# Project a layer's first five units from tiles without their 1/rms factor and scale the results; let two buffer pairs change roles

## What is computed

```python
for l in range(DEPTH):
    u = rmsnorm(h, norm_g[l])                       # h * rsqrt(mean(h*h) + eps) * g
    p = u @ w_in[l]                                 # 1024 x 9216
    hq, hf_f, hf_b, hi, hgt, aq, ak, av, agt = split(p)
    o_h = hgrn2_mixer(hq, hf_f, hf_b, hi, hgt, lbs[l], hg_norm_g[l])
    o_a = diff_attention_mixer(aq, ak, av, agt, ...)
    h = h + concatenate([o_h, o_a]) @ w_out[l]      # 2048 x 1024
out = rmsnorm(h, final_norm_g)
```

## Time and profile before

| | |
|---|---|
| median of 3 runs | 1586.7 us (1586.59 to 1586.84) |
| the profiled execution, its own time | 1587.1 us |
| its span, first to last instruction | 1585.3 us |
| PE busy | 1496.3 us (94%) |
| DVE busy | 986.5 us (62%) |
| ACT busy | 772.8 us (49%) |
| POOL busy | 533.2 us (34%) |
| mean granted TensorE clock | 0.988 of full |

### The profile page before, as it was taken

How to read it: one execution, slowest core, us unless ns; L and a number is a source line. 1 busy time by engine, 2 the same in 40 slices (tenths; PEclk the granted TensorE clock), 3 DMA queues, 4 the chain that set the end, 5 groups by cost and what they waited for, 6 DMA issues and landing times.

```text
span 1585.3 us, 27727 instructions
## 1 busy us (share of the span) xinstructions
PE 1496.3 (94%) x11148; PEld 1412.5 (89%) x11148; DVE 986.5 (62%) x1542; ACT 772.8 (49%) x1689; POOL 533.2 (34%) x287
## 2 busy tenths in 40 slices
PE   5999999999999999999979999999999999999986
PEld 4999999999999999998879999999998898888874
DVE  6666677676734666666465666676676356665655
ACT  5445444554434555555434544445444345565542
POOL 2323322333333333333333333333333343333331
PEclk8999999999999999999989999999999999999999
DMA  4221111211223222222122121221212232222221
GB/s 155 81 67 55 54 58 63 68 55 54 68 68 94 68 68 68 67 65 66 59 67 75 60 67 54 67 63 58 68 54 67 67 96 79 67 71 78 74 62 66
DMA packets 34480, 109.39 MB, mean 69 GB/s; under 512 B 4912, under 2 KB 5040, under 8 KB 34352
## 3 DMA queue, kind: packets, MB, share of 16 engines
q1 hardware_dynamic: 34352, 107.61, 21.9%
HBM read 96.84 MB, written 2.10 MB: 62 GB/s over the span
## 4 chain that ended last, share of the span: by engine, by line
PE 76%; DVE 13%; issue 6%; ACT 2%; DMA 1%; POOL 1%; SPq 1%; DVEq 0%; ACTq 0%; POOLq 0%
PE proj L1247 51%; PE pair L1316 7%; PE meta L1426 3%; PE pair L1411 2%; PE pair L1413 2%; PE main L1440 2%; DVE stage L969 1%; PE main L1381 1%; DVE totals L1030 1%; PE main L1382 1%; DMA q_stack<-gate_f 1%; PE pair L1362 1%; DVE neg_max L1160 1%; DVE o_rows L1104 1%; PE main L1323 1%
## 5 line engine op out<-in xcount | busy, mean ns | idle before, releaser
L509 POOL TENSOR_TENSOR w_lo<-w_raw,w_hi 128x1024 fp32r<-128x1024 f32 x178 | 441.9, 2484 | 753.9 <-ACT w_hi L568 752.1
L1247 PE MATMUL proj<-u_hi,w_hi 128*128 128x264 f32 (+1 forms) x2048 | 497.0, 314 | 15.2 <-DVE u_lo L923 15.2
L1247 PE MATMUL proj<-u_hi,w_lo 128*128 128x264 f32 (+1 forms) x2048 | 466.8, 300 | 0.0
L1247 PE MATMUL proj<-u_lo,w_hi 128*128 128x264 f32 (+1 forms) x2048 | 466.8, 299 | 0.0
L1247 PEld LDWEIGHTS proj<-u_hi,w_hi 128*128 128x128 f32 x2048 | 329.4, 191 | 27.9 <-issue 16.3
L1247 PEld LDWEIGHTS proj<-u_hi,w_lo 128*128 128x128 f32 x2048 | 327.3, 189 | 11.1
L1247 PEld LDWEIGHTS proj<-u_lo,w_hi 128*128 128x128 f32 x2048 | 327.9, 190 | 7.6
L1160 DVE TENSOR_REDUCE neg_max<-pair 128x1 f32<-128x528 f32 (+1 forms) x144 | 101.3, 704 | 226.7 <-PE pair L1413 226.6
L743 ACT ACTIVATE decay<-pair,neg_max 128x528 f32<-128x528 f32 (+1 forms) x144 | 100.7, 699 | 253.9 <-DVE neg_max L1160 253.9
L568 ACT ACTIVATE w_hi<-w_raw 128x1024 fp32r<-128x1024 f32 x178 | 186.6, 1049 | 22.2 <-DMA w_raw<-w_units 11.9
L689 ACT ACTIVATE qk_dec<-ops 128x528 f32<-128x528 f32 (+1 forms) x112 | 75.8, 677 | 126.1 <-DVE ops L1057 126.1
(11 more groups left out here) (182 smaller groups left out, 2253.4 us busy)
## 6 DMA issues: line engine op xcount, KB each, us to landing
w_raw<-w_units SPq DMA_DIRECT2D x178, 512.0 KB, 3.5
k_stack<-k_stack SPq DMA_DIRECT2D x32, 132.0 KB, 2.3
q_stack<-gate_f SPq DMA_DIRECT2D x32, 132.0 KB, 2.4
h<-x_t SPq DMA_DIRECT2D x8, 264.0 KB, 4.7
out_t<-decay SPq DMA_DIRECT2D x4, 256.0 KB, 2.1
out_t<-ops SPq DMA_DIRECT2D x4, 256.0 KB, 2.1
cos_sin<-rope SPq DMA_DIRECT2D x1, 528.0 KB, 5.5
masks<-level_masks SPq DMA_DIRECT2D x1, 448.0 KB, 5.3
```

Source lines behind the costliest of these rows:

```text
L509: pool.tensor_tensor(w_lo[:, u % N_CUT, :, :], w_raw[:, u % N_RAW, :, :], w_hi[:, u % N_CUT, :, :].bitcast(f32), ALU.subtract)\
L1247: ins = pe.matmul(out, w, x[:, k, cols_n], start=(k == 0 and p == 0), stop=(k == last_k and p == 2))
```

## The change

The first five units of a layer take h * g, without 1/rms, as their operand. Its high and low parts are cut on ACT (`cut_raw_high`) and DVE (`cut_raw_low`) and lie in the buffers that hold the mixed heads of that layer later; the two pairs of buffers (u and mixed) change roles from layer to layer. In layer 1 the raw tiles are cut in the tail of layer 0. DVE multiplies each of the five results by 1/rms as it takes it from PSUM (`scale_first`), and ACT's sigmoids then read the staged tile (`gate_first`). The tiles of u, which units 5 and later need, are made between these steps as `FIRST_CUTS` says: two, three and three tiles behind the scaling of zb, q and v. The sum of squares moves behind piece 7 of unit 0 (layer 0) or piece 4 of unit 0 (layer 1). In layer 0 the transfers change order: gain, tile 0, weights 0, tile 1, weights 1, the other tiles, small constants; the masks and the rotary tables follow behind weights 2, under a semaphore of their own.

```diff
+FIRST_CUTS = ((), (0, 1), (2, 3, 4), (5, 6, 7), ())
+RAW_AFTER = {OUT_C: range(EARLY_TILES + 2), OUT_C + 1: (EARLY_TILES + 2,), OUT_C + 2: (EARLY_TILES + 3,)}
...
+        u_of = ((even_hi, even_lo), (odd_hi, odd_lo))
+        mix_of = ((odd_hi, odd_lo), (even_hi, even_lo))
...
+            def cut_raw_high(l, k):
...
+                wait_tile(act, l, k)
+                act.activation(mix_of[l][0][:, tile, :], h[:, tile, :], ACT.Copy, scale=g_in[:, l, tile:tile + 1])\
+                    .then_inc(raw_hi_ready, 1)
...
+            def gate_first(l, i):
...
+                if what in ("zf", "zb", "g"):
+                    use = l * HEADS * 3 + STAGE_USE[what]
+                    act.wait_ge(evacuated[t % 2], evac_count(t))
+                    a, b = (stage[:, use % 2, x, tokens(l, what)] for x in range(2))
+                    if what == "g":
+                        act.activation(a, b, ACT.Sigmoid).then_inc(first_gated, 1)
+                    else:
...
+                        w = step(act.activation(b, a, ACT.Sigmoid, scale=-1.0))
+                        act.activation(a, a, ACT.Sigmoid).then_inc(first_gated, 1)
...
+                        act.activation(ops[:, c % 2, (KF, KB)[d], :], b, ACT.Copy,
+                                       scale=one_minus_lb[:, l, row:row + 1]).then_inc(k_scaled, 1)
+                act.wait_ge(unit_done, t + 1)
+                cut_high(t + N_CUT)
...
             for k in range(KT):
+                cut_raw_high(0, k)
+                if k < 2:
+                    cut_high(k)
                 square_h(0, k)
-            cut_high(0)
+            cut_high(2)
             root(0)
...
                 for i in range(len(HG_TILES)):
-                    evacuate(l, i)
+                    gate_first(l, i)
+                    for k in FIRST_CUTS[i]:
+                        cut_u(l, k)
...
+            def cut_raw_low(l, k):
...
+                dve.scalar_tensor_tensor(raw_lo[:, tile, :], h[:, tile, :], g_in[:, l, tile:tile + 1],
+                                         raw_hi[:, tile, :].bitcast(f32), ALU.mult, ALU.subtract)\
+                    .then_inc(raw_lo_ready, 1)
...
+            def scale_first(l, i):
...
+                dve.wait_ge(unit_done, t + 1)
...
+                dve.tensor_tensor(rows_of(l, what, dst), grown(l, what, proj[t % 2]), rows_of(l, what, sq),
+                                  ALU.mult).then_inc(evacuated[t % 2], 1)
...
             for k in range(KT):
+                cut_raw_low(0, k)
+                if 1 <= k < KT - 1:
+                    add_squares(0, k)
+            prepare_exponents()
             for l in range(DEPTH):
-                norm_u(l)
...
+                invert_roots(l)
+                for i in range(len(HG_TILES)):
+                    scale_first(l, i)
+                    if l == i == 0:
+                        prepare_lower_bounds()
+                    if i == 2:
+                        follow(l, 0)
+                        follow(l, 1)
+                        start_operands(l, 0)
+                    for k in FIRST_CUTS[i]:
+                        norm_u(l, k)
+                        if k > 0:
+                            cut_u_low(l, k - 1)
+                    if i == len(HG_TILES) - 2:
+                        cut_u_low(l, KT - 1)
...
-                for k in range(KT + 1):
-                    if k < KT:
+                if l == 0:
+                    for k in range(KT):
                         piece(l, 0, k)
-                    if k > 0:
-                        piece(l, 1, k - 1)
+                        if k == KT - 1:
+                            sum_squares(l)
+                        piece(l, 1, k)
+                else:
+                    for k in range(KT):
+                        piece(l, 0, k)
+                        if k == KT // 2:
+                            sum_squares(l)
+                    for k in range(KT):
+                        piece(l, 1, k)
```

More of the change, by code:

```diff
@@ L368, in encoder_trunk, with tile_order, wait_tile @@
         dve_step = sem("dve_step")
+        def tile_order(l):
+            return TILE_ORDER if l > 0 else tuple(range(KT))
+        def wait_tile(eng, n, k):
+            tile = tile_order(n)[k]
+            if n == 0:
+                eng.wait_ge(x_in[tile], 16)
+            elif tile < EARLY_TILES - 1:
+                eng.wait_ge(last_added, (n - 1) * (EARLY_TILES - 1) + tile + 1)
+            else:
+                t = (n - 1) * LAYER_UNITS + (OUT_C if tile == EARLY_TILES - 1 else unit_of(tile))
+                eng.wait_ge(evacuated[t % 2], evac_count(t))
         halves = (slice(0, HALF), slice(HALF, T))
@@ L614, in evacuate @@
                     use = (l * HEADS + c) * 3 + STAGE_USE.get(what, 0)
-                    if what in HG_TILES and l * HG_HEADS + c > 0:
+                    if what in HG_TILES:
                         act.wait_ge(k_scaled, 2 * (l * HG_HEADS + c))
@@ new lines, in norm_u, with cut_u_low @@
+            def norm_u(l, k):
+                if k >= 4:
+                    dve.wait_ge(u_lo_ready, l * KT + k - 4 + 1)
+                dve.scalar_tensor_tensor(decay[:, k % 4, :], h[:, k, :], g_in[:, l, k:k + 1], sq[:, :],
+                                         ALU.mult, ALU.mult).then_inc(u_ready, 1)
+            def cut_u_low(l, k):
+                dve.wait_ge(u_hi_ready, l * KT + k + 1)
+                u_hi, u_lo = u_of[l]
+                dve.tensor_tensor(u_lo[:, k, :], decay[:, k % 4, :], u_hi[:, k, :].bitcast(f32), ALU.subtract)\
+                    .then_inc(u_lo_ready, 1)
@@ L1239, in piece @@
                 last_k = (EARLY_K if OUT_B <= i < OUT_LATE else KT) - 1
-                if i == 0:
-                    pe.wait_ge(u_lo_ready, l * KT + k + 1)
-                hi, lo = (mix_hi, mix_lo) if what in ("outA", "outB") else (u_hi, u_lo)
-                wh, wl = w_hi[:, t % N_CUT, k, :], w_lo[:, t % N_CUT, k, :]
+                tile = k
+                if i < len(HG_TILES):
+                    tile = tile_order(l)[k]
+                    hi, lo = mix_of[l]
+                    pe.wait_ge(raw_lo_ready, l * KT + k + 1)
+                else:
+                    hi, lo = (mix_of if what in ("outA", "outB") else u_of)[l]
+                    if i == len(HG_TILES):
+                        pe.wait_ge(u_lo_ready, l * KT + k + 1)
+                wh, wl = w_hi[:, t % N_CUT, tile, :], w_lo[:, t % N_CUT, tile, :]
                 for w, x, p in ((wh, hi, 0), (wh, lo, 1), (wl, hi, 2)):
```

146 lines of the change are left out of this document (85 added, 61 removed).

## The result

The changed kernel takes 1589.87 us (median of 16 runs, 1588.95 to 1592.55), the kernel before 1586.9 us (16 runs, 1585.44 to 1589.04). The ratio is 1.0019 with a 95% interval of 1.0011 to 1.0027: 3 us more. The profiled execution after took 1590.38 us, its span is 1588.6 us. The forecast was 1590.0 us.

A forecast was written before the change was run, and what follows sets the result against it. TensorE bound the kernel (three quarters of the last chain); VectorE's chain, held by weight cuts, would set level 1: +3.0 (layer 0) - 3.5 (layer 1) + 2 x 2.0 (clock) = +3.5 us, so 1590.0 us, range 1578 to 1595.

The forecast's parts named there:

- The holes at the heads: Head of each layer: TensorE's waits for u's low half, 8.6 us in layer 0 and 6.6 in layer 1, go.
- The opening: Start of layer 0: squares summed at 25.0, 1/rms ready at 31.35 instead of 19.0, 12.3 us later.
- The rival of a still later opening: Layer 0: 1/rms comes at 33 to 35 and all behind it moves, 1592 to 1595 us; chance 0.23.
- VectorE's chain: From 1/rms to level 1: VectorE's serial work, lengthened by weight cuts, sets level 1; layer 0 at 63.0.
- the hold: Ahead of level 1: four GpSimd weight cuts hold VectorE 2.3 us each, 9.2 in layer 0, 8.1 in layer 1.
- The rival in which VectorE isn't held: Both layers up to level 1: TensorE stays the bound, 1574 us; chance 0.10, with 0.10 more for half the holds.
- Layer 0: Up to level 1 of layer 0: level 1 at 63.0 against 60.01, 3.0 us later (bounds 1 and 5).
- the clock: Behind level 1 in each layer: TensorE's idleness lets its clock fall, adding 2.0 us (bounds 0 and 2.6).
- Layer 1: Up to level 1 of layer 1: level 1 at 857.1 against 860.61, 3.5 us earlier (bounds 1.5 and 6).
- the idleness of VectorE: Layer 1, ahead of the scaling of unit 1: 3 us VectorE can't use, since its order is written out.
- The rival in which the clock doesn't fall: Behind level 1 in both layers: no slow stretch, +3.0 - 3.5 = -0.5, 1586 us, no change; chance 0.17.
- The end: Behind level 1 and at the kernel's end: nothing changes, 0 us.

The follow-up runs named there:

- no holds: Changed kernel with GpSimd's low cuts of weight units 3 to 6 of each layer on one of eight tiles: 1577.16 us.
- both fillers: Changed kernel with 20, then 10, extra matmul calls whose result nobody reads, on TensorE ahead of its wait at level 1 in both layers: 1594.44 and 1587.18 us.
- early keys: Changed kernel with ScalarE's key copy for level 1 moved to the step of unit q, ahead of the scaling of g, in both layers: 1586.13 us.
- the version with all edits: Changed kernel with key copy early, layer 0's square sum behind piece 4, cuts of u moved forward, g's product behind the widening for level 2: 1579.25 us.
- the early sum alone: Changed kernel with layer 0's sum of squares behind piece 4 of unit 0 instead of piece 7: 1586.09 us.
- layer 1 alone: Changed kernel with layer 0 and the order of the transfers as before the change, so only layer 1 is changed: 1586.09 us.
- the half filler: Changed kernel with 10 extra matmul calls whose result nobody reads, on TensorE ahead of its wait at level 1 in both layers: 1587.18 us.

## Why the prediction was right

**The holes at the heads: right.** Both waits for u_lo are gone. In layer 0 another of 4.3 us came in their place, for the scaling of unit 0 (forecast: 4).

**The opening: right, but 1.1 us too long.** The sum of squares started at 24.07, not at 25.0. The sum as it is written gives another number than its result: four pieces at 1.32 and eleven at 0.73 from 13.0 end at 26.3. 25.0 comes out when the first slow piece, which could start at 10.0, is left out. Seen so, most of the difference is the start: unit 1's first piece came at 12.26 and not at 13.0, and from there the matmuls went from 0.64 us to 0.41 at 15.5 (see the rows above). The second cut weight was there at 12.2 (forecast 12.95), the raw tiles at 22.0 (23.1). By the rate of 0.39 MB per us the two weight units would have landed at 6.0 and 8.0, not at 6.4 and 8.5; ScalarE began to cut them at 5.49 and 8.71. Sum and root took 2.72 us (2.82), the reciprocal 3.45 (3.45). The rival of a still later opening has fallen. But 1.1 us is no more than this opening varies: in the four experiments that leave it as it is (no holds, both fillers, early keys) the reciprocal of layer 0 starts at 26.90, 27.21, 27.88 and 28.14. The last of them is ready at 31.59, behind the forecast.

**VectorE's chain: right, with the hold a little too long.** From 1/rms to level 1 in layer 0 it was 30.97 us; 31.65 had been worked out. There are four held operations in each layer, as forecast. With 0.7 us for a free norm or low cut and 0.55 for a free L1069, the four of layer 0 lost 2.2 + 2.2 + 1.9 + 2.1 = 8.4 us against 9.2. This one term accounts for the difference, and it could have been read from the rows: 3.53 against 1.4 and 2.67 against 0.43 are 2.1 and 2.2 us of loss, not 2.3. In layer 1 these were 7.3 us (833.92, 837.36, 840.37 and 852.16) against 8.1. The rule of the Trainium skill, page "SBUF — State Buffer", section "SBUF: two separate sides", as the prediction tells it, agrees with three of the four in layer 0: the norms and the low cut have two SBUF inputs, and the last two of them ended at 40.33 and 55.35, behind the weight cuts that ended at 39.76 and 54.78. The gate at 42.02 has one full-width input only and was held all the same, until 44.43 beside a cut that ended at 44.13. With the cuts shortened the kernel is 12.7 us faster. The rival in which VectorE isn't held had 1574 us; taking the holds out gave 1577.16, and with them in, the rival has fallen.

**Layer 0: the sum was 1.8 us too high.** Forecast +3.0 at level 1 and +2.0 for the clock; measured +1.2 and +2.0 (3.87 us between the levels before, 5.91 after). The 1.8 are the opening with 1.1 and the chain with 0.7. From level 2 to the tail of layer 0 another 0.4 came. Of it 0.3 lies where the granted clock is 0.91 in 740:760 after and 1.00 in the same stretch before: the weight cuts at 741.14 and 764.15 before stand 3.36 and 3.67 us later after.

**Layer 1: right.** Taken from the shift of 3.66 with which layer 0 ends, the marks came where they were worked out: the reciprocal ready at 825.8 (825.95), the scaling of unit 1 at 829.64 (829.75), level 1 at 857.2 (857.1). The timeline after, with that shift in it:

```profile
826.00 3.45 DVE L977 RECIPROCAL mixed_t<-mixed_t 128x528 f32<-128x528 f32 x1 [0.87 <-ACT mixed_t L631]
...
833.30 0.71 DVE L1022 TENSOR_TENSOR stage<-proj,mixed_t 128x528 f32<-128x528 f32 x1 [3.10 <-PE proj L1370]
...
860.87 2.04 PE L1440 MATMUL pair<-ops,qk_dec 128*128 128x128 f32 x8 [5.04 <-ACT qk_dec L747]
...
866.16 1.12 PE L1440 MATMUL pair<-ops,qk_dec 128*128 128x128 f32 x8
```

The 3.10 us at 833.30 are the idleness of VectorE that the forecast said it can't use; the version with all edits uses it. Levels 1 and 2 are 1.75 us further apart than before (5.29 and 3.54), where 2.0 were forecast for the clock; by the filler 1.3 of it is the clock. The rival in which the clock doesn't fall has fallen with the two fillers.

**The end: wrong.** I had said that nothing changes behind level 1. Up to the weight cut that stands at 1489.61 before, the shift stays near 2.0 us, but at the end it is 3.3. Windows of the last heads and of the last output projection, first of the kernel before, then of the kernel after:

```profile
1500.00:1525.00 25.00, 22.33 (x120) 18.30 (x119) 12.41 (x20) 12.72 (x31) 8.80 (x6) 0.93 0.23 64
1538.00:1558.00 20.00, 16.41 (x72) 12.84 (x71) 8.23 (x9) 7.21 (x11) 11.37 (x7) 1.00 0.18 53
```

```profile
1504.00:1529.00 25.00, 21.86 (x124) 17.47 (x123) 14.73 (x20) 12.13 (x31) 9.71 (x6) 1.00 0.18 52
1542.00:1562.00 20.00, 16.41 (x66) 12.69 (x65) 9.00 (x9) 6.98 (x10) 10.00 (x7) 0.91 0.16 53
```

Before, the clock is low for a while in the attention of the last head (0.93), where TensorE also waits for others. After, it is full there and low in the output projection (0.91), between 1547 and 1558, where TensorE works without a wait. In 1542:1562 66 matmuls are counted where the same stretch before has 72. Over the first place the shift of the weight cuts falls from 2.05 us (the one at 1507.92 before) to 1.69 (1523.81), over the second it rises from 1.68 (1542.17) to 3.22 (1554.10). From level 2 of layer 1 to the last reciprocal it is 709.9 us before and 711.1 after. So 1.2 us come from a slow stretch that changed its place. The profiled executions with the early keys alone, the early sum alone and layer 1 alone have it at the late place too, the half filler has it at neither, the others have it at the early one. Why it lies here in one and there in another is open. That slow stretches differ from one execution to the next of the same kernel can be said, though: the mean granted clock of the 16 executions after is 0.986 or 0.987 in seven and 0.989 to 0.991 in nine, and the medians of the two groups are 1590.48 and 1589.36 us; the profiled execution (0.986) is of the first. The 55 of the kernel before that stand beside the experiments have 0.986 to 0.994 and show no such difference (medians 1586.6 us below 0.990 and 1586.8 above 0.991). A difference of 1 us between two of these medians is therefore not read as one of the edits.

The total of +3.3 us between the two spans is thus 1.2 + 2.0 + 0.4 in layer 0, 1.65 less in layer 1, and 1.3 in the rest; the medians are 3.0 apart. The forecast of +3.5 had 5.0, 1.5 less, and 0. It came out as close as it did because a term too high by 1.8 met two that were missing, 0.4 and 1.3, both for the most part slow stretches that nothing in the forecast knew of. That is luck. Without it the forecast would have been off by under 2 us.

## What to carry to other kernels

Before you take a serial step off the bound engine's path, add up the program of the engine that gets the work, up to the next mark where the bound engine needs it. An order written out by hand turns every operation ahead of the needed one into latency. Where TensorE is full, an idle stretch costs itself and a slower stretch behind it: 4.7 us of waiting had another 2 behind it here, and filling the waits with products that nobody reads gave 2.7 us back. And count how many operations of the moved work fall beside GpSimd's, since here each of these lost some 2 us on top of its own 0.7.

## What was not expected of the hardware

A float32 matmul call makes two instructions: 20 calls were 40 instructions and 9.06 us, 0.23 us each (264 columns, granted clock 1.00). The fp32r matmuls of the projection take a unit of 48 in 5.87 us, 0.12 us each.

Which of VectorE and GpSimd stands goes by who is under way. Beside the weight cut at 51.73 (3.05 us, shown above) stood, before the norm step that was held:

```profile
51.18 0.76 DVE L993 SCALAR_TENSOR_TENSOR decay<-h,g_in,mixed_t 128x528 f32<-128x528 f32 x1
...
51.86 0.70 DVE L1000 TENSOR_TENSOR even_lo<-decay,even_hi 128x528 fp32r<-128x528 f32 x1
```

Both took what they take when free, and it is the weight cut that was 0.7 us longer than the 2.35 of the one at 61.52 in the trace with the early keys. That one began when VectorE's operation before had 0.15 us left and 0.06 us ahead of the next, at 61.58; there VectorE's took 2.86 us and the cut lost nothing. So in these rows a weight cut that starts while VectorE works is longer by about the rest of that work, and the operation of VectorE that comes once the cut is under way is held.

ScalarE loads its activation table ahead of the wait for the operand here. In layer 1 after, the load stands directly behind the root and beside the reciprocal, and the first sigmoid follows the scaling with no load between:

```profile
825.99 1.28 ACT L658 ACT_TABLE_LOAD   x1
...
830.23 0.65 ACT L658 ACTIVATE stage<-stage 128x528 f32<-128x528 f32 x1 [2.96 <-DVE stage L1022]
```

So the change of tables, which could have been a further 1.28 us in the chain, cost nothing.
